# A fifth Strassen block product in the first couples of a transformer layer's MLP, with the mixtures taken two units later

## What is computed

```python
u = rms_norm(h, norm_mlp_g)
h = h + jnp.square(jax.nn.relu(u @ mlp_w1)) @ mlp_w2      # mlp_w1: 2048 x 8192, mlp_w2: 8192 x 2048
```

## Time and profile before

| what | value |
|---|---|
| median of 3 runs (lowest, highest) | 1180.3 us (1180.22, 1180.61) |
| profiled execution: time | 1180.27 us |
| its span | 1178.5 us |
| PE busy | 1171.6 us, 99% of the span |
| DVE busy | 848.4 us, 72% |
| ACT busy | 641.8 us, 54% |
| mean granted TensorE clock | 0.999 of full |
| HBM traffic over the span | 211 GB/s |

### The profile page before, as it was taken

How to read it: one execution, slowest core, us unless ns; L and a number is a source line. 1 busy time by engine, 2 the same in 40 slices (tenths; PEclk the granted TensorE clock), 3 DMA queues, 4 the chain that set the end, 5 groups by cost and what they waited for, 6 DMA issues and landing times.

```text
span 1178.5 us, 14344 instructions
## 1 busy us (share of the span) xinstructions
PE 1171.6 (99%) x5396; PEld 974.3 (83%) x5396; DVE 848.4 (72%) x1159; ACT 641.8 (54%) x896; POOL 22.5 (2%) x31
## 2 busy tenths in 40 slices
PE   9999999999999999999999999999999999999998
PEld 7888888888888888888888888888888888888886
DVE  6568876888766678855789864989666799576544
ACT  6745455666655556643466543565633566455432
POOL 1000100000000000000000000000000000000000
PEclk9999999999999999999999999999999999999999
DMA  9867764334348666885467875477865477876741
GB/s 346 320 179 235 225 232 144 108 108 127 107 158 267 220 231 211 275 267 193 143 224 240 287 249 196 129 232 243 298 239 177 163 242 255 280 232 211 266 165 36
DMA packets 110981, 249.26 MB, mean 212 GB/s; under 512 B 9664, under 2 KB 55744, under 8 KB 110912
## 3 DMA queue, kind: packets, MB, share of 16 engines
q1 hardware_dynamic: 110768, 248.34, 63.5%
q10 hardware_dynamic: 144, 0.01, 0.0%
HBM read 233.63 MB, written 14.68 MB: 211 GB/s over the span
## 4 chain that ended last, share of the span: by engine, by line
PE 99%; DMA 0%; DVE 0%; SPq 0%; ACT 0%; issue 0%
PE acc L1842 59%; PE acc L1867 11%; PE sc L1842 7%; PE tr L1867 7%; PE sc L1867 6%; PE sc L2070 1%; PE sc L2035 1%; PE tr L1987 1%; PE tr L1977 0%; PE sc L1977 0%; PE tr L2123 0%; PE tr L2122 0%; DMA w_raw<-in_nsa_w_in_units_dram 0%; PE acc L1959 0%; PE tr L2099 0%; PE tr L2100 0%
## 5 line engine op out<-in xcount | busy, mean ns | idle before, releaser
L1219 DVE TENSOR_TENSOR w_split<-w_raw,w_split 128x1024 fp32r<-128x1024 f32 x226 | 271.0, 1219 | 103.6 <-ACT w_split L774 103.0
L774 ACT ACTIVATE w_split<-w_raw 128x1024 fp32r<-128x1024 f32 x226 | 232.3, 1054 | 109.4 <-PE acc L1842 96.9
L1842 PE MATMUL acc<-w_split,a_hi 128*128 128x512 f32 x908 | 283.7, 393 | 0.7 <-DVE w_split L1214 0.7
L1842 PE MATMUL acc<-w_split,b_split 128*128 128x512 f32 x1044 | 244.9, 391 | 0.0
L1842 PEld LDWEIGHTS acc<-w_split,b_split 128*128 128x128 f32 x1044 | 194.9, 188 | 40.0
L1842 PEld LDWEIGHTS acc<-w_split,a_hi 128*128 128x128 f32 x908 | 167.5, 188 | 35.4 <-issue 1.4
L1842 PE MATMUL acc<-w_split,a_lo 128*128 128x512 f32 x454 | 177.0, 390 | 0.0
L1219 DVE TENSOR_TENSOR t_split<-w_raw,t_split 128x1024 fp32r<-128x1024 f32 x70 | 84.4, 1221 | 42.5 <-ACT t_split L774 42.2
L1842 PE MATMUL acc<-t_split,b_split 128*128 128x512 f32 x492 | 114.3, 389 | 0.0
L1842 PEld LDWEIGHTS acc<-t_split,b_split 128*128 128x128 f32 x492 | 92.3, 188 | 19.2
L1842 PEld LDWEIGHTS acc<-w_split,a_lo 128*128 128x128 f32 x454 | 85.2, 188 | 18.2
(11 more groups left out here) (280 smaller groups left out, 1594.6 us busy)
## 6 DMA issues: line engine op xcount, KB each, us to landing
w_raw<-in_mlp_w_units_dram SPq DMA_DIRECT2D x256, 512.0 KB, 4.4
w_raw<-in_nsa_w_in_units_dram SPq DMA_DIRECT2D x76, 512.0 KB, 4.6
w_raw<-in_nsa_w_out_units_dram SPq DMA_DIRECT2D x32, 512.0 KB, 4.3
w_raw<-in_ple_w_gate_units_dram SPq DMA_DIRECT2D x32, 512.0 KB, 5.7
turn_dram<-v_slc SPq DMA_DIRECT2D x44, 128.0 KB, 3.5
turn_dram<-v_win SPq DMA_DIRECT2D x44, 128.0 KB, 3.1
v_slc<-turn_dram SPq DMA_DIRECT2D x22, 256.0 KB, 4.8
v_win<-turn_dram SPq DMA_DIRECT2D x22, 256.0 KB, 4.4
```

What stands on the lines that cost most here:

```text
L774: nc.scalar.activation(hi, w_raw[:, u % RAW], ACT.Copy).then_inc(hi_done, 1)
L1219: nc.vector.tensor_tensor(lo, w_raw[:, u % RAW], f32(hi), ALU.subtract).then_inc(lo_done, 1)
L1842: last = nc.tensor.matmul(banks_of(c)[t][:], xs[:, kt, toks], ws[:, m * NW:(m + 1) * NW], start=(kt == 0 and n == 0), stop=(kt == KT - 1 a ...
```

## The change

The set of quads gets k = 2, so first couples have quads at k = 2 to 6; second couples keep 4, 5, 6. The buffer `mixed` (4 blocks) becomes a function: blocks 0 and 1 lie in `stage`, 2 and 3 in a new `mixed_two`. The combined rows grow from 4 to 5 per kind. In first couples `keep_one` and `mix` move from s = 15 of the couple to s = 1 of the second couple. What is left out of the diff is every further `mixed[:, m]` turned into `mixed(m)`.

```diff
-QUADS = (3, 4, 5, 6)
+QUADS = (2, 3, 4, 5, 6)
 N_QUADS = len(QUADS)
...
-REST = max(8, 40 + 4 * UW + 8 * NW + 8 * N_QUADS * P
+REST = max(8, 40 + 6 * UW + 2 * NW + 8 * N_QUADS * P
...
-                    nc.sbuf_tensor("mixed", [P, 4, NW], F32) as mixed:
+                    nc.sbuf_tensor("mixed_two", [P, TT, NW], F32) as mixed_two:
...
+        def mixed(m):
+
+            return stage[:, m] if m < TT else mixed_two[:, m - TT]
...
                 for s in split_hi_pair(c):
-                    if s == 2 * UPC - 1:
+                    if p and s == 2 * UPC - 1:
                         keep_one(c)
+                    if p and q and s == 1:
+                        keep_one(c - 2)
...
                 for s in split_lo_pair(c):
-                    if s == 2 * UPC - 1:
+                    if p and s == 2 * UPC - 1:
                         mix(c)
+                    if p and q and s == 1:
+                        mix(c - 2)
```

More of the change, by code:

```diff
@@ L805, in keep_one @@
                     act.wait_ge(blocks_turned, TT * (T_HID + (c - C_MLP) // 8 * 4 + (c - C_MLP) % 8))
-                nc.scalar.activation(mixed[:, 0], mixes[0][:], ACT.Copy).then_inc(one_copied, 1)
+                nc.scalar.activation(mixed(0), mixes[0][:], ACT.Copy).then_inc(one_copied, 1)
             def hidden_out(c, half):
@@ L811, in hidden_out @@
                 for t in range(TT):
-                    src = mixed[:, 2 * half + t]
+                    src = mixed(2 * half + t)
                     act.wait_ge(summed, 4 * n + 2 * half + t + 1)
@@ L1283, in mix @@
                 dve.wait_ge(one_copied, n + 1)
-                nc.vector.tensor_tensor(mixed[:, 3], six[:], mixed[:, 0], ALU.subtract).then_inc(mix_step, 1)
+                nc.vector.tensor_tensor(mixed(3), six[:], mixed(0), ALU.subtract).then_inc(mix_step, 1)
                 dve.wait_ge(mix_step, 2 * n + 1)
-                nc.vector.tensor_tensor(mixed[:, 2], five[:], mixed[:, 3], ALU.add)
-                nc.vector.tensor_tensor(mixed[:, 1], seven[:], mixed[:, 3], ALU.add).then_inc(mix_step, 1)
+                nc.vector.tensor_tensor(mixed(2), five[:], mixed(3), ALU.add)
+                nc.vector.tensor_tensor(mixed(1), seven[:], mixed(3), ALU.add).then_inc(mix_step, 1)
                 dve.wait_ge(mix_step, 2 * n + 2)
-                nc.vector.tensor_tensor(mixed[:, 3], five[:], mixed[:, 1], ALU.add).then_inc(mix_ready, 1)
+                nc.vector.tensor_tensor(mixed(3), five[:], mixed(1), ALU.add).then_inc(mix_ready, 1)
             def pair_sums(c):
@@ L1296, in pair_sums @@
                 for m, bank in enumerate((c11, c21, c12)):
-                    nc.vector.tensor_tensor(mixed[:, m], bank[:], mixed[:, m], ALU.add).then_inc(summed, 1)
-                nc.vector.tensor_tensor(mixed[:, 3], c22[:], mixed[:, 3], ALU.subtract).then_inc(summed, 1)
+                    nc.vector.tensor_tensor(mixed(m), bank[:], mixed(m), ALU.add).then_inc(summed, 1)
+                nc.vector.tensor_tensor(mixed(3), c22[:], mixed(3), ALU.subtract).then_inc(summed, 1)
             def turn_hidden(n):
@@ L1305, in turn_hidden @@
                 else:
-                    turn_blocks(n, lambda t: mixed[:, 2 * ((n - T_HID) % 2) + t])
+                    turn_blocks(n, lambda t: mixed(2 * ((n - T_HID) % 2) + t))
             def transposed_lo(r, hi, lo, kt0, gain, i=0, banks=(0, 1)):
```

## The result

The changed kernel takes 1185.72 us (median of 4 runs, 1185.19 to 1186.03), the kernel before 1180.28 us (1180.22 to 1180.61): a ratio of 1.0045, 95% interval 1.0033 to 1.0058. It is slower by 5.4 us; 1185.3 us were forecast. Among all executions behind this document two ran at a much lower granted clock (1473.7 us at 0.75 for the kernel before, 1978.2 us at 0.556 for the one with fourth quads) and stand in no ratio.

The account below looks back on a forecast made before the run. The prediction took PE to bound the kernel, with DVE's head start deciding whether PE waits. It summed -2.04 us of matmuls and +7.11 us of stalls to +5.07 us, 1185.3 us, range 1183.1 to 1187.8 us for 8 in 10.

Parts of the forecast that it names:

- What bounds the kernel: MLP first couples: PE never waits; DVE loses 1.84 us per quad against PE and lives on its head start.
- Fewer matmuls: Three first couples: one more pair each in 21 matmuls in place of 24, 2.04 us off PE.
- DVE's quad of 6.60 us: First couples: DVE needs 6.60 us from one quad's own units to the next's, without idling; PE needs 4.76 us.
- anchor: End of `down` in quarter 2: additions to `h` at 736.59, first sums 737.79, first own units 740.38; claimed not to move.
- The stalls: PE waits for T0 in each first couple: 0.53 us at k = 4, 1.84 us at k = 5; 7.11 us in three.
- The sum: Whole kernel: -2.04 + 7.11 = +5.07 us on 1180.27 us, giving 1185.3 us, 0.4% slower.
- Late mixtures: Begin of second couples: mixtures two units later are there 0.7 us before PE wants them; cost nothing.
- Larger rows: Quarter 0: larger combined rows add 1.6 us of DVE behind 5 us of cover; nothing, without cover at most 1.6 us.
- DVE keeping up: Rival at T0 of k = 5: DVE 2.4 us earlier, no slowdown, 1178.2 us; chance 0.10.
- Mixtures too late: Rival: same stalls, and PE also waits at the begin of second couples, 1187.7 to 1190.1 us; chance 0.07.
- The clock: Rival: clock falls to 1.2 GHz behind the stalls, one quad after each second stall at that level, 1199.6 us; chance 0.03.

Follow-up runs that it names:

- the one with fourth quads: Early sums plus a fourth quad (k = 3) in all four second couples: 1183.60 us, ratio 1.0027 to the kernel before.
- early sums: Changed kernel with the sums of each first couple's first quad in `stage` and `mixed_two`, additions to `h` behind that quad's first low part: 1178.20 us.
- two runs: Mixtures of first couples back at s = 15, once in the changed kernel (1185.17 us), once in early sums (1178.22 us).

## Why the prediction was right, point by point

- *What bounds the kernel*: right, PE paces it and DVE's head start decides.
- *Fewer matmuls*, 3 x 0.68 us: shown by the couples without stalls (40.12 us with early sums, against 40.80).
- *DVE's quad of 6.60 us*, its anchor 1.2 us behind the begin of the additions, T0 4.33 us behind the own units: all as read before, to 0.01 us.
- *The stalls*: 0.53 and 1.84 us forecast, 0.34 + 0.12 = 0.46 and 1.71 + 0.12 = 1.83 measured, at the items named. PE's restart was priced from its one wait at the kernel's begin, 0.14 us behind DVE and 0.08 us slow; in mid-stream it is 0.05 and 0.12 us. The two errors cancel to 0.1 us a couple, which is luck. k = 6 had no stall, k = 3 none either.
- *The sum*: +5.07 us forecast; the trace has 4.9 in the couples, which is what the sum is about, and the medians 5.4 (interval 3.9 to 6.8 us).
- *Late mixtures, cost nothing*: right. The last addition ended at 780.01; PE began the second couple's weight loads at 780.56. What the text did not ask was whether they are needed; two runs show that they are not.
- *Larger rows*: 1.6 us of DVE behind cover: `r_split` took 2.82 us, 0.53 more than in the earlier trace rows, and PE did not wait: quarter 0's couple lasted 41.48 us in both kernels.
- *The rivals*: DVE keeping up fell with the six waits; its condition, sums that do not wait for the end of `down`, was built and gave just its time (1178.2 us). Mixtures too late: no wait there. The clock stayed at 1.00, its 2.4 GHz level, in the windows around stalls of 1.7 us. What a longer idle time does to it, no run here shows.

## What to carry to other kernels

When an edit trades work on the busy engine for work on one that feeds it, compare the two rates in the stretch (here 4.76 against 6.60 us a quad) and then the head start; shares of the span hide both. A head start is lost to what the feeding engine has to wait for at the stretch's begin: here a buffer laid over another, and moving the first 2.6 us of sums into free buffers, with one low part behind them, turned +5.4 us into -2.2. Helping a loaded VectorE from GpSimd can make it slower, since its operations with two SBUF inputs became longer beside GpSimd's.

## What the runs showed of the hardware that was not expected

A 128x512 addition in float32 took 0.69 us on VectorE; on GpSimd it took 1.30 us beside transposes of VectorE and 2.20 us beside VectorE's operations with two SBUF inputs, of which it stretched the second from 1.22 to 2.31 us. PE goes on 0.05 us after the end of the VectorE operation that it waited for, and its first three matmuls then take 0.80 us in place of 0.68.
